# A network of four blocks in one launch: first chunks multiplied ahead of the norm's root, weight splits moved, latent projections reordered

## The reference

```python
xf * lax.rsqrt(jnp.mean(xf * xf, axis=-1, keepdims=True) + EPS)   # rms_norm, then times g

# first_block
h = rms_norm(x, g_mix[l])
z = jnp.einsum("bsd,de->bse", h, w_in[l]) + b_in[l]
va, ga, xb, gb, sa, sb = jnp.split(z, cuts, axis=-1)
u = va * jax.nn.sigmoid(ga)                       # then a causal convolution of 31 taps
... # v: a convolution of 4 taps on xb and a gated recurrence, times gelu(gb)
x = x + jnp.einsum("bsd,de->bse", m, w_o[l])
# second_block: hgrn2_mixer (8 heads), then the latents of the attention
ckr = hn @ w_dkv
c_kv = rmsnorm(ckr[..., :MLA_KV_LORA], kv_norm)   # 256 wide
k_rope = apply_rope(ckr[..., MLA_KV_LORA:], cos, sin)
c_q = rmsnorm(xn @ w_dq, q_norm)                  # 256 wide
```

## Time and profile before

| | |
|---|---|
| device time, median of 3 runs | 2377.82 us (2376.51 to 2377.89) |
| device time of the profiled execution | 2375.6 us |
| its span | 2373.8 us |
| granted TensorE clock, mean | 0.985 |
| busy: TensorE / VectorE / ScalarE / GpSimd | 96% / 49% / 37% / 36% |

### The profile page before, as it was taken

How to read it: one execution, slowest core, us unless ns; L and a number is a source line. 1 busy time by engine, 2 the same in 40 slices (tenths; PEclk the granted TensorE clock), 3 DMA queues, 4 the chain that set the end, 5 groups by cost and what they waited for, 6 DMA issues and landing times.

```text
span 2373.8 us, 29772 instructions
## 1 busy us (share of the span) xinstructions
PE 2279.3 (96%) x10216; PEld 1823.1 (77%) x10216; DVE 1160.5 (49%) x1784; ACT 879.9 (37%) x1097; POOL 862.5 (36%) x189
## 2 busy tenths in 40 slices
...
GB/s 131 89 100 96 88 59 49 72 57 103 98 101 94 88 93 101 70 55 71 70 36 89 100 88 101 93 88 77 65 32 49 36 72 89 89 93 102 88 88 106
DMA packets 232942, 193.95 MB, mean 82 GB/s; under 512 B 18224, under 2 KB 228656, under 8 KB 232880
## 3 DMA queue, kind: packets, MB, share of 16 engines
...
## 4 chain that ended last, share of the span: by engine, by line
issue 46%; PE 41%; POOL 11%; ACT 1%; DVE 1%; POOLq 0%; DMA 0%; DVEq 0%; SPq 0%; ACTq 0%
POOL w_lo L537 11%; PE ps L1548 9%; PE ps L1549 9%; PE ps L1550 9%; PE ps L1581 2%; PE ps L1582 2%; PE ps L1583 2%; PE ps L1975 2%; PE ps L1952 1%; PE ps L1953 1%; PE ps L1964 1%; ACT w_hi L558 0%; PE ps L1557 0%; PE ps L1558 0%; PE ps L1559 0%
## 5 line engine op out<-in xcount | busy, mean ns | idle before, releaser
L537 POOL TENSOR_TENSOR w_lo<-raw,w_hi 128x2048 fp32r<-128x2048 f32 x184 | 860.5, 4677 | 1482.6 <-ACT w_hi L558 1482.6
L558 ACT ACTIVATE w_hi<-raw 128x2048 fp32r<-128x2048 f32 x184 | 351.1, 1909 | 533.2 <-PE ps L1550 290.9
L1548 PE MATMUL ps<-XH,w_hi 128*128 128x512 f32 x1128 | 448.7, 398 | 3.1 <-DVE XL L357 3.1
L1550 PE MATMUL ps<-XH,w_lo 128*128 128x512 f32 x1128 | 446.0, 395 | 0.0
L1549 PE MATMUL ps<-XL,w_hi 128*128 128x512 f32 x1128 | 446.0, 395 | 0.0
L1548 PEld LDWEIGHTS ps<-XH,w_hi 128*128 128x128 f32 x1128 | 211.8, 188 | 56.9 <-DVE XL L357 3.8
L1549 PEld LDWEIGHTS ps<-XL,w_hi 128*128 128x128 f32 x1128 | 211.9, 188 | 52.8 <-issue 1.4
L1550 PEld LDWEIGHTS ps<-XH,w_lo 128*128 128x128 f32 x1128 | 211.7, 188 | 51.8
L1201 DVE TENSOR_TENSOR X<-X,ps 128x512 f32 x72 | 49.6, 688 | 339.8 <-PE ps L1550 176.8
L1581 PE MATMUL ps<-XH,w_hi 128*128 128x512 f32 x448 | 185.9, 415 | 19.1 <-DVE XL L332 10.2
L693 ACT ACTIVATE FH<-tmp 128x512 f32 (+1 forms) x96 | 60.8, 633 | 372.2 <-DVE tmp L1187 372.2
...
## 6 DMA issues: line engine op xcount, KB each, us to landing
...
```

Of the source, the lines that this page charges most:

```text
L537: pool.tensor_tensor(w_lo[:, s], raw[:, s], w_hi[:, s].bitcast(F32), ALU.subtract)\
L558: act.activation(w_hi[:, s], raw[:, s], ACT.Copy).then_inc(hi_done, 1)
L1548: pe.matmul(dst, his[k], xh[k], start=start and k == 0, stop=False)
L1550: mm = pe.matmul(dst, los[k], xh[k], start=False, stop=stop and k == n - 1)
```

## The change

Four parts.

**Start.** SyncE loads the vectors, chunk 0 and `ones` ahead of x, and x in four quarters (two feature tiles each), chunk 1 behind it. TensorE transposes four tiles, multiplies chunk 0 by their parts as they come, and transposes the others in between; PSUM banks for the transposed tiles are 2 to 7. The parts are of x times gain without the root: ScalarE writes XHU from PSUM with the gain as its scale, VectorE XLU from the same bank (`low_half`) and a copy X (`keep_x`), in the order low 0, 1, X 0, 1, low 2 to 5, X 2, 3, low 6, 7, X 4 to 7. Chunks 0 to 3 are multiplied by XHU and XLU. The squares are now taken by ScalarE on the token-major x (four activations over 1024 elements, each with its sum), which gives the root on 128 partitions x 4; VectorE puts it on a diagonal (`tensor_scalar` of `ident`), and a product with ones spreads it over the partitions (in the midst of chunk 1). VectorE then multiplies the eight columns of chunks 0 to 3 by the root, and ScalarE adds bias or takes the sigmoid in place. XH and XL with the root are formed between these, for chunk 4 on.

**Heads 0 and 7.** In head 0 the split of the next odd chunk moves from behind the exponentials to ahead of the seven HE exponentials. In head 7 the split of the last chunk moves ahead of OH. Heads 1 to 6 stay.

**Latents.** kvq's chunks now hold both tiles of w_dq in c, then the keys' tiles in c+1 and c+2, one each. `one_tile` makes all w_hi products first, then an optional other step, then waits for w_lo. The ones product of the queries stands within the second tile of the keys, that of the keys within the rope tile, the rope swap among the attention's first queries; ScalarE's and VectorE's steps follow that order.

The diff, cut to its core (shifted left; removed: the functions `norm_act` and `norm_pe` and counts of semaphores; `norm_dve` now calls `between()` ahead of tile 4 and otherwise does the same; "ug" is `plain(..., begun=2)`):

```diff
     sp.dma_start(ident[:], a["ident"]).then_inc(ident_in, 16)
-    for h in range(2):
-        cols = slice(h * 512, h * 512 + 512)
+    sp.dma_start(vec[:], a["vectors"]).then_inc(consts_in, 16)
+    def load_x(h):
+        cols = slice(h * 256, h * 256 + 256)
         sp.dma_start(x_tm[:, :, cols], a["x"][:, :, cols].rearrange("b (t p) d -> p (b t) d", p=P)).then_inc(x_in[h], 16)
-    sp.dma_start(vec[:], a["vectors"]).then_inc(consts_in, 16)
-    sp.dma_start(ones[:], a["ones"]).then_inc(consts_in, 16)
...
     c = FIRST["ug"]
-    with sp.Fori(0, 4) as i:
+    load8(c, 0, w_in, 0)
+    sp.dma_start(ones[:], a["ones"]).then_inc(consts_in, 16)
+    for h in range(4):
+        load_x(h)
+    load8(c + 1, 1, w_in, D)
+    with sp.Fori(1, 4) as i:
...
     c = FIRST["kvq"]
-    load1(c, 0, a["mla_w_dq_2"], 0, 8)
-    load1(c + 1, 1, a["mla_w_dq_2"], P, 8)
-    load8(c + 2, 0, a["kv_w_dkv_2"], 0)
+    load8(c, 0, a["mla_w_dq_2"], 0)
+    load1(c + 1, 1, a["kv_w_dkv_2"], 0, 8)
+    load1(c + 2, 0, a["kv_w_dkv_2"], P, 8)
...
+    split_hi(0, 0)
+    act.wait_ge(consts_in, 32)
     for k in range(KD):
         act.wait_ge(s_("x_turned"), k + 1)
-        act.activation(X[:, k], ps[:, k % 4], ACT.Copy).then_inc(s_("x_fm"), 1)
-    norm_act(act, "n_mix", lambda k: (s_("x_fm"), k + 1), first=lambda: (split_hi(0, 0), split_hi(1, 1)))
+        act.activation(XHU[:, k], ps[:, X_BANKS[k]], ACT.Copy, scale=col("g_mix", k)).then_inc(s_("xu_hi"), 1)
+    split_hi(1, 1)
+    n = "n_mix"
+    for b in range(TB):
+        act.activation(GA[:, 2 * b:2 * b + 2].rearrange("p a t -> p (a t)"), x_tm[:, b], ACT.Square,
+                       accum_out=small[:, 96 + b:97 + b]).then_inc(sig(n, "sq"), 1)
+    act.preload_act_table_set(LN_EXP)
+    act.wait_ge(*at(n, "sq", TB))
+    act.activation(small[:, 100:104], small[:, 96:100], ACT.Ln, bias=col("eps"), scale=1.0 / D)\
+        .then_inc(sig(n, "ln"), 1)
+    act.wait_ge(*at(n, "ln", 1))
+    act.activation(small[:, 104:108], small[:, 100:104], ACT.Exp, scale=-0.5).then_inc(sig(n, "inv"), 1)
...
     c = FIRST["ug"]
-    with act.Fori(0, 4) as i:
+    def columns_scaled(i, js):
+        for j in js:
+            dst = (CO, GA)[j // 2][:, 2 * i + j % 2]
+            act.wait_ge(s_("z_scaled"), 4 * i + j + 1)
+            act.activation(dst, dst, (ACT.Identity, ACT.Sigmoid)[j // 2],
+                           bias=col("b_in", 2 * i + KD * (j // 2) + j % 2)).then_inc(ev, 1)
+    def scaled_hi(ks):
+        for k in ks:
+            act.wait_ge(*at("n_mix", "t", k + 1))
+            act.activation(XH[:, k], tmp[:, 2 + k % 2], ACT.Copy).then_inc(sig("n_mix", "hi"), 1)
+    split_hi(c + 2, 0)
+    columns_scaled(0, (0, 1))
+    scaled_hi(range(4))
+    split_hi(c + 3, 1)
+    columns_scaled(0, (2, 3))
+    scaled_hi(range(4, KD))
+    for s in range(2):
+        columns_scaled(1, (2 * s, 2 * s + 1))
+        split_hi(c + 4 + s, s)
+    with act.Fori(2, 4) as i:
...
         act.activation(HKD[:, n], HKD[:, n], ACT.Exp).then_inc(s_("h_kd_e"), 1)
+        if first:
+            split_hi(c + 3, 1)
...
             root_out(h - 1)
-        if more:
+        if not first:
             split_hi(2 * h + c + 3, 1)
-        if not first:
             out_act(h - 1)
         if more:
             split_hi(2 * h + c + 4, 0)
-        else:
-            split_hi(2 * h + c + 3, 1)
...
         scaled_act(act, "n_kv", k, at("mlp1", "dn", 28 + k + 1), "kv_in_norm_2", 0, XH2)
+    act.preload_act_table_set(LN_EXP)
     split_hi(c + 2, 0)
-    rest_act(act, "n_kv")
-    split_hi(c + 3, 1)
+    act.wait_ge(*at("n_kv", "mean", 1))
+    inverse_act(act, "n_kv", D)
...
-        act.preload_act_table_set(LN_EXP)
         inverse_act(act, n, LORA, W[:, 6])
+        if n == "ckv":
+            split_hi(c + 5, 1)
...
     small_squares("cq", CQ)
+    split_hi(c + 3, 1)
+    small_rest("cq", CQ, CQH)
     split_hi(c + 4, 0)
-    small_rest("cq", CQ, CQH)
     small_squares("ckv", CK)
-    split_hi(c + 5, 1)
...
     lam.put(dve.tensor_tensor(ab, nl, col("lam", 0, 12), ALU.max))
-    norm_dve(dve, "n_mix", "g_mix")
+    def low_half(k):
+        dve.wait_ge(s_("xu_hi"), k + 1)
+        dve.scalar_tensor_tensor(XLU[:, k], ps[:, X_BANKS[k]], col("g_mix", k), XHU[:, k].bitcast(F32), ALU.mult,
+                                 ALU.subtract).then_inc(s_("xu_lo"), 1)
+    def keep_x(k):
+        dve.tensor_copy(X[:, k], ps[:, X_BANKS[k]]).then_inc(s_("x_fm"), 1)
...
+    dve.wait_ge(*at("n_mix", "inv", 1))
+    for b in range(TB):
+        dve.tensor_scalar(tmp[:, 0, b * P:(b + 1) * P], ident[:], small[:, 104 + b:105 + b], None, ALU.mult)\
+            .then_inc(s_("r_diag"), 1)
+    dve.wait_ge(*at("n_mix", "mean", 1))
+    dve.tensor_copy(rst[:, 1], ps[:, 7]).then_inc(s_("r_row"), 1)
+    dve.wait_ge(s_("r_row"), 1)
+    def columns_scaled(i, js):
+        for j in js:
+            dve.wait_ge(halves, half_at(2 * i + j // 2, j % 2))
+            dve.tensor_tensor((CO, GA)[j // 2][:, 2 * i + j % 2], ps[:, j], rst[:, 1], ALU.mult)\
+                .then_inc(s_("z_scaled"), 1)
+    columns_scaled(0, (0, 1))
+    norm_dve(dve, "n_mix", "g_mix", lambda: columns_scaled(0, (2, 3)))
+    columns_scaled(1, range(4))
...
-    small_copy("cq", CQ, 4, [half_at(c), half_at(c + 1)])
-    small_copy("ckv", CK, 0, [half_at(c + 2, 0), half_at(c + 2, 1)])
+    small_copy("cq", CQ, 0, [half_at(c), half_at(c)])
     small_norm_dve("cq", CQ, "mla_q_norm_2", CQH, CQL)
+    small_copy("ckv", CK, 4, [half_at(c + 1), half_at(c + 2)])
...
     kc.put(dve.tensor_tensor(KR[:], QR[:, 2], cos_t[:], ALU.mult))
+    small_norm_dve("ckv", CK, "kv_norm_2", CKH, CKL)
     dve.wait_ge(s_("kr_swap"), 1)
-    kc.put(dve.tensor_tensor(CK[:, 7], ps[:, 3], sin_t[:], ALU.mult))
+    kc.put(dve.tensor_tensor(CK[:, 7], ps[:, 6], sin_t[:], ALU.mult))
...
-    pe.wait_ge(consts_in, 32)
-    norm_pe(pe, "n_mix")
-    def plain(c, iters, ev, xh, xl, ready=None):
-        with pe.Fori(0, iters) as i:
+    def turn_x(k):
+        pe.wait_ge(x_in[k // 2], 16)
+        if k >= 6:
+            pe.wait_ge(s_("x_fm"), k - 5)
+        for b in range(TB):
+            mm = pe.transpose(ps[:, X_BANKS[k], b * P:(b + 1) * P], x_tm[:, b, k * P:(k + 1) * P], ident[:])
+    def first_hi(ks):
+        pe.wait_ge(hi_done, 1)
+        for k in ks:
+            pe.wait_ge(s_("xu_lo"), k + 1)
+            for n in range(2):
+                w = w8(w_hi, 0, n)[k]
+                pe.matmul(ps[:, n], w, XHU[:, k], start=k == 0, stop=False)
+                pe.matmul(ps[:, n], w, XLU[:, k], start=False, stop=False)
+    def first_lo(ks):
+        chunk_in(0)
+        for k in ks:
+            for n in range(2):
+                mm = pe.matmul(ps[:, n], w8(w_lo, 0, n)[k], XHU[:, k], start=False, stop=k == KD - 1)
+    for k in range(4):
+        turn_x(k)
+    first_hi(range(2))
+    for k in range(4, 6):
+        turn_x(k)
+    first_hi(range(2, 4))
+    for k in range(6, KD):
+        turn_x(k)
+    first_lo(range(4))
+    first_hi(range(4, KD))
+    first_lo(range(4, KD))
+    chunk_in(1)
+    pe.wait_ge(s_("x_fm"), KD)
+    half8(1, 0, 2, XHU, XLU)
+    pe.wait_ge(s_("r_diag"), TB)
+    for b in range(TB):
+        mm = pe.matmul(ps[:, 7, b * P:(b + 1) * P], ones[:], tmp[:, 0, b * P:(b + 1) * P], start=True, stop=True)
+    mm.then_inc(sig("n_mix", "mean"), 1)
+    half8(1, 1, 3, XHU, XLU)
+    for j in range(2):
+        chunk_in(2 + j)
+        pe.wait_ge(s_("z_evac"), 4 + 2 * j + 2)
+        half8(j, 0, 2 * j, XHU, XLU)
+        half8(j, 1, 2 * j + 1, XHU, XLU)
+    def plain(c, iters, ev, xh, xl, ready=None, begun=0):
+        with pe.Fori(begun, iters) as i:
...
-    def one_tile(c, s, bank, xh, xl, ready=None):
-        chunk_in(c)
+    def one_tile(c, s, bank, xh, xl, ready=None, middle=None):
+        pe.wait_ge(hi_done, c + 1)
         h, l = w1(w_hi, s, 8), w1(w_lo, s, 8)
         for k in range(KD):
...
-            mm = product(ps[:, bank], [h[k]], [l[k]], [xh[:, k]], [xl[:, k]], start=k == 0, stop=k == KD - 1)
-            if k in (KD // 2 - 1, KD - 1):
-                mm.then_inc(halves, 1)
+            pe.matmul(ps[:, bank], h[k], xh[:, k], start=k == 0, stop=False)
+            pe.matmul(ps[:, bank], h[k], xl[:, k], start=False, stop=False)
+        if middle is not None:
+            middle()
+        chunk_in(c)
+        for k in range(KD):
+            mm = pe.matmul(ps[:, bank], l[k], xh[:, k], start=False, stop=k == KD - 1)
+        mm.then_inc(halves, 2)
...
-    one_tile(c, 0, 4, XH, XL, lambda k: at("n_mla", "lo", k + 1))
-    one_tile(c + 1, 1, 5, XH, XL)
+    chunk_in(c)
+    pe.wait_ge(*at("mlp1", "dn", 34))
+    pair(0, 0, XH, XL, lambda k: at("n_mla", "lo", k + 1))
     squares_pe(pe, "n_kv")
-    chunk_in(c + 2)
+    one_tile(c + 1, 1, 4, XH2, XL2, lambda k: at("n_kv", "lo", k + 1))
+    one_tile(c + 2, 0, 5, XH2, XL2, middle=lambda: small_norm_pe("cq", CQ))
     pe.wait_ge(*at("mlp1", "dn", 36))
-    pair(0, 0, XH2, XL2, lambda k: at("n_kv", "lo", k + 1))
```

(20 more changed lines are left out.)

70 lines of the change are left out of this document (29 added, 41 removed).

## The result

The changed kernel took 2353.1 us (median of four runs, 2351.7 to 2356.9), the kernel before 2377.6 beside it: 0.9903 of its time, 95% interval 0.9891 to 0.9915. A second series beside other runs of before gave 2355.0 against 2377.1, 0.9906 (0.989 to 0.9923). So it is about 1% (22 to 24 us) faster, where 34.0 us were forecast. Both times are slower than the forecast proper (2340.6 to 2348); the first lies just inside the slow edge of the range (2353.5), the second outside it. The profiled execution took 2354.3 us with a span of 2352.4; it is compared with the 2375.6 of before, 21.3 us less.

What follows compares the result with a forecast made beforehand. TensorE, busy 2279 of 2373.8 us, was taken as the bound, so only pauses, slow clock and order could give time. Terms 14.0 - 0.9 + 4.1 + 16.8 = 34.0 us took 2377.8 to 2343.8 us; range 2335 to 2353.5.

Steps and rivals of the forecast that it cites:

- the forecast proper: Whole kernel: the main predicted interval of the measured time, 2340.6 to 2348 us, chance 0.48.
- The start: Up to the Gelu: chunk 4 starts at 60.4 instead of 77.6 us, gain 17.2, less 3.2; net 14.0 us.
- The Gelu's pause: Before the third gb chunk: VectorE's later convolution delays the Gelu columns, costing 3.2 us, between 0 and 5.
- Head 0: Earlier split: two successive w_lo hold VectorE's HQD and HKD behind it, HKD reaching TensorE at 1003.1; loss 0.9 us.
- the first rival: Head 0 and Gelu: VectorE gets the port (4.2 us), Gelu not late (up to 3.2); 2336.4 to 2340.6, chance 0.2.
- Head 7: Earlier last split removes the 4.47 us pause; level 1 waits 1.8 us for HV without slow clock; gain 4.1 us.
- The latents: From 1652.14 to 1713.04 us: pauses and low clock of 19.4 us shrink to small new waits; gain 16.8 us, give or take 3.
- Just in time is too late: Thin margins at chunk 1, chunk 4 and the latents' splits, or late x, are missed; 2348 to 2354 us, chance 0.28.
- The port and the convolution are kinder: VectorE gets the port in head 0 and the Gelu isn't late; 2336.4 to 2340.6 us, chance 0.2.
- The clock doesn't rise: At the start: TensorE stays at 1.2 GHz through four chunks, costing 37.2 us; 2380.8 us, chance 0.01.
- nothing at the end: Removed waits return at the Gelu, head 0 and keys, as VectorE's or ScalarE's chain keeps its time; 2373 to 2382, chance 0.02.
- the things that the prediction said would show it: Trace signs: start times, Gelu pause about 3 us, HQD some 8, head 7's HV pause under 2, latents' pauses at most 2.

Runs made afterwards that it cites:

- lam_early: The changed kernel with VectorE's small operations on lam moved into its idle time ahead of the root's row; 2351.4 us, ratio 0.989.
- x_behind_6: The changed kernel with VectorE's X times gain times FR of head 6 placed behind OL; 2350.6 us, ratio 0.9889.
- credits_early: The changed kernel with ScalarE's four credits for the attention's PSUM banks given ahead of the keys' squares, not behind the keys' high parts; 2348.2 us, ratio 0.9877.

## Why the prediction was right or wrong

**The start: 11.6 for 14.0.** The steps up to the first product held: transposes at 9.85 (9.6), first XHU product at 13.15 (13.0). Chunk 0 then took 14.1 us instead of 12.9, and here the step failed. Up to 15.00 its products came 0.43 us apart, the pace of the low level, and behind that 0.23 to 0.35:

```profile
14.15 0.63 PE L1650 MATMUL ps<-XHU,w_hi 128*128 128x512 f32 x1
14.58 0.63 PE L1651 MATMUL ps<-XLU,w_hi 128*128 128x512 f32 x1
15.00 0.51 PE L1650 MATMUL ps<-XHU,w_hi 128*128 128x512 f32 x1
15.35 0.39 PE L1651 MATMUL ps<-XLU,w_hi 128*128 128x512 f32 x1
15.58 0.40 PE L1650 MATMUL ps<-XHU,w_hi 128*128 128x512 f32 x1
```

The full pace came 5.2 us after the transposes began, where the sum had it after 3.4. The granted clock reads 1.00 in this stretch, in before's as well, so slow clock is read from the pace alone here. Chunk 4 stood at 61.87 instead of 60.4. The Gelu's pause was 3.18 for 3.2, and lam_early shows its cause to be the one named. What the sum also put at nothing is the slow clock behind it, 1.4 us for the seven products of the window, though the prediction itself said, in a rival, that a pause over 3 us slows the clock. UP came at 70.66 (69.6), and one operation on lam stood still for 4.55 us, as expected.

**Head 0: the number right, the mechanism wrong in a detail.** The pause (8.60) and the loss (0.9) came as forecast; who got the port between the two w_lo did not. By the prediction's own words it is wrong "if HQD in head 0 takes under 4 us", and it took 3.84, with 4.98 for HKD. That the sum is the same is in part luck: the sum had HQD held over both w_lo, the first rival had VectorE let in and 4.2 us gained, and neither asked what the second w_lo does to HKD, for which TensorE waits.

**Head 7: 1.3 for 4.1.** The hold on X was forecast (5.05 for 5.11), but its first victim was taken to be OH and HV, and the wait at the levels to be 1.8 us without slow clock. The failed step is the list of who waits: the diagonal writes the bank that tmp reads, and it comes before the levels. The price was 2.74 us of pause and 14 instructions in 3.4 us at 0.50 of the clock; x_behind_6 took both away.

**The latents: 9.5 for 16.8.** This is the term that put the sum off most. The small pauses went, as forecast. Of the 7.90 us that the earlier trace rows gave as ended by ScalarE's queue at L878, the failed step left 1.15: it followed VectorE's chain (KR, al_done), and put at nothing what that row names, a semaphore increment (a credit) in ScalarE's order, behind CKH. In the new order it still stood behind CKH, and CKH still behind a VectorE operation beside a w_lo. The wait measured 7.33 us, with 1.8 of slow clock behind it for the first nine products. credits_early gives 7.8 us back with one line moved, which is about the whole miss of 7.3.

**The rivals.** "Just in time is too late" named the right time, 2348 to 2354, and for the most part a wrong place. Chunk 1 was just in time (its w_lo ended at 27.21, its first product began at 27.27, at most 0.2 late); no margin at chunk 4 or at the latents' w_lo was missed. Right in it was only that slow clock follows a pause. Of "The port and the convolution are kinder" the first condition came true and gained nothing, since HKD was held in HQD's place. "The clock doesn't rise" and "nothing at the end" did not occur. Of the things that the prediction said would show it, three failed: HQD, the 2.74 us in head 7 (under 2 expected, and at HV), and no pause over 2 us in the latents (7.33).

**The arithmetic.** Two figures are off by a little and change nothing: 2343.8 and 37.2 us for a clock that doesn't rise make 2381.0, not 2380.8, and from HKD at 1003.1 to HKD at 998.6 it is 4.5 us, where the sum is said to end 4.2 lower.
